# A hybrid DeltaNet and attention block: own buffers for the x rows, small rows on ACT's queue, early k-tiles four pieces sooner, block products of the two scan directions alternating

## What is computed

```python
shift, scale, gate = jnp.split((jax.nn.silu(c) @ w_mod + b_mod)[:, None, :], 3, axis=-1)
shift_c, scale_c, gate_c = jnp.split(jax.nn.silu(c_ctx) @ w_mod + b_mod, 3, axis=-1)
h = rms_norm(x, norm_w) * (1.0 + scale) + shift
hc = rms_norm(ctx, norm_w) * (1.0 + scale_c) + shift_c
aq, ak, av, az, ab, aa, bq, bk, bv, bz, br = split_in(h @ w_in)      # and the same for hc
# A: short conv, silu, l2 norm; gated delta rule in both directions, context first
#    each chunk solves (I + L) u = b v - ..., then o = q S + (q k^T decay) z, S <- g S + k^T z
# B: grouped-query attention with rotary positions over context and latent keys
x_new = x + gate * (sig(br_a) * (a_lat @ w_proj_a) + sig(br_b) * (b_lat @ w_proj_b)) @ w_out
```

## Time and profile before

| | us |
|---|---|
| median of 3 runs | 1854.47 |
| lowest and highest run | 1850.68, 1855.86 |
| the profiled execution | 1851.49 |
| its span, first to last instruction | 1849.2 |
| PE busy in the span | 1781.2 |
| DVE, ACT, POOL busy | 947.0, 661.9, 277.5 |

### The profile page before, as it was taken

The page is one execution under the profiler, slowest core; times in us unless marked ns, Lnnn a source line. Parts: engine busy times, 40 slices in busy tenths (PEclk is TensorE's granted clock), DMA queues, the critical chain, the costliest instruction groups (busy, mean ns, idle before and its releaser), DMA issues.

```text
span 1849.2 us, 25568 instructions
## 1 busy us (share of the span) xinstructions
PE 1781.2 (96%) x10286; PEld 1456.5 (79%) x10286; DVE 947.0 (51%) x1662; ACT 661.9 (36%) x1212; POOL 277.5 (15%) x421
## 2 busy tenths in 40 slices
PE   5799999999999999999999999999998999999999
PEld 2367888888787888878888888877877788788887
DVE  1244443456423566645555553764457876463334
ACT  4323331223233555535424345422246444222121
POOL 0000000000003356576100002111100110210000
PEclk9899999999999999999999999999999999999999
DMA  8794212223224566655444436767633332752332
GB/s 299 255 326 125 66 52 63 57 69 91 64 68 134 175 198 177 191 169 154 132 137 134 117 111 193 224 203 219 182 106 105 92 103 91 267 184 101 115 124 102
DMA packets 198685, 267.13 MB, mean 144 GB/s; under 512 B 37072, under 2 KB 135625, under 8 KB 197161
## 3 DMA queue, kind: packets, MB, share of 16 engines
q1 hardware_dynamic: 175241, 192.74, 34.7%
q0 software_dynamic: 15552, 58.62, 9.5%
q10 hardware_dynamic: 7776, 14.16, 2.1%
HBM read 221.96 MB, written 43.52 MB: 144 GB/s over the span
## 4 chain that ended last, share of the span: by engine, by line
PE 82%; DVE 7%; DMA 4%; ACT 4%; issue 2%; POOL 1%; SPq 0%; ACTq 0%; DVEq 0%; POOLq 0%
PE psum L1671 23%; PE psum L1673 22%; PE psum L1672 22%; PE psum L1819 2%; DMA w_raw_mod<-w_mod_dram 1%; PE psum L1768 1%; PE psum L1770 1%; DVE w_lo L1099 1%; PE psum L1664 1%; PE psum L1776 1%; ACT w_hi L765 1%; PE psum L1772 1%; PE psum L1774 1%; DMA w_raw<-w_proj_b_dram 1%; PE psum L1998 1%
## 5 line engine op out<-in xcount | busy, mean ns | idle before, releaser
L1099 DVE TENSOR_TENSOR w_lo<-w_raw,w_hi 128x1024 fp32r<-128x1024 f32 x232 | 291.0, 1254 | 593.0 <-ACT w_hi L765 592.7
L765 ACT ACTIVATE w_hi<-w_raw 128x1024 fp32r<-128x1024 f32 x232 | 245.7, 1059 | 861.6 <-PE psum L1673 772.3
L1671 PE MATMUL psum<-h_hi,w_hi 128*128 128x512 f32 x1152 | 469.6, 408 | 7.7 <-DVE w_lo L1099 5.4
L1672 PE MATMUL psum<-h_lo,w_hi 128*128 128x512 f32 x1152 | 451.6, 392 | 0.0
L1673 PE MATMUL psum<-h_hi,w_lo 128*128 128x512 f32 x1152 | 451.0, 392 | 0.0
L1671 PEld LDWEIGHTS psum<-h_hi,w_hi 128*128 128x128 f32 x1152 | 217.5, 189 | 67.0 <-issue 19.4
L1673 PEld LDWEIGHTS psum<-h_hi,w_lo 128*128 128x128 f32 x1152 | 216.9, 188 | 47.6
L1672 PEld LDWEIGHTS psum<-h_lo,w_hi 128*128 128x128 f32 x1152 | 217.8, 189 | 35.9
L1169 DVE SCALAR_TENSOR_TENSOR conv_acc<-conv_in,convw,conv_acc 128x772 f32<-128x772 f32 x96 | 98.2, 1023 | 3.4
L1671 PE MATMUL psum<-w_hi,m_hi 128*128 128x512 f32 x256 | 99.6, 389 | 0.0
L1672 PE MATMUL psum<-w_lo,m_hi 128*128 128x512 f32 x256 | 99.6, 389 | 0.0
(11 more groups left out here) (323 smaller groups left out, 2860.0 us busy)
## 6 DMA issues: line engine op xcount, KB each, us to landing
w_raw<-w_in_dram SPq DMA_DIRECT2D x168, 512.0 KB, 3.9
w_raw_mod<-w_mod_dram SPq DMA_DIRECT2D x64, 512.0 KB, 5.8
w_raw_modg<-w_mod_dram POOLq DMA_DIRECT2D x32, 512.0 KB, 4.7
w_raw<-w_out_dram SPq DMA_DIRECT2D x32, 512.0 KB, 3.7
gate_scratch<-gate_stage ACTq DMA_DIRECT2D x48, 256.0 KB, 4.3
w_raw<-w_proj_a_dram SPq DMA_DIRECT2D x16, 512.0 KB, 4.1
w_raw<-w_proj_b_dram SPq DMA_DIRECT2D x16, 512.0 KB, 3.5
gates<-gate_scratch POOLq DMA_DIRECT2D x32, 256.0 KB, 4.2
```

The source lines that it names most:

```text
L765: act.activation(part(whi[i % 2], p), part(place, p), ACT.Copy).then_inc(S("w_hi"), 1)
L1099: dve.tensor_tensor(part(wlo[i % 2], p), part(raw_of(n)[0], p), part(whi[i % 2], p).bitcast(f32), ALU.subtract).then_inc(S("w_lo"), 1)
L1671: pe.matmul(out_ap, lh, rh, start=first, stop=False, skip_group_check=shared)
L1672: pe.matmul(out_ap, lh, rl, start=False, stop=False, skip_group_check=shared)
```

## The change

1. Each of the six x tiles gets a buffer of its own, four of them in parts of `h_hi` and `h_lo` that aren't written yet. POOL loads tile t when tile t-2 has landed, and starts once the five transfers into `rows` have landed. A tile is taken up every two pieces instead of every three; its transposes come four pieces after its squares instead of three.
2. The ring of mod buffers has six places instead of four.
3. The six small transfers are issued by ACT instead of SP. PE waits for five of them; conv_rows is transposed after mod piece 3 and copied by DVE two pieces later.
4. Every early piece stands four mod pieces sooner (27, 35, 43, 51, 59 instead of 31, 39, 47, 55, 63), with its loads and splits. The conv piece after mod piece 63 (`BRIDGE`) gives its first k-tile before the last `mod_cols`.
5. `mod_cols` comes one piece later, at the second piece after a group's last one, `mod_columns` behind it; the first `h_columns` no longer waits until five pieces after the last x tile's squares.
6. In couple5, correct5, couple6 and correct6 PE first waits for both directions and then alternates between them head by head; `gp0` comes with the last but one product, `gp1` with the last.

```diff
-EARLY = {31: (0, 0), 39: (1, 0), 47: (0, 1), 55: (1, 1), 63: (0, 2)}
+EARLY = {27: (0, 0), 35: (1, 0), 43: (0, 1), 51: (1, 1), 59: (0, 2)}
...
+    BRIDGE = MOD_AT[63] + 1
+    BEFORE_LAST = {MOD_AT[63]: (BRIDGE, 0)} | {MOD_AT[m - 6 + 2 * kk]: (MOD_AT[m] + 1, kk) for m in EARLY for kk in range(3)}
     SPLIT_AT = [n - 1 for n in range(NP)]
     for m in EARLY:
-        SPLIT_AT[MOD_AT[m] + 1] = MOD_AT[m - 10]
-    SPLIT_AT[MOD_AT[63] + 2] = MOD_AT[59]
+        SPLIT_AT[MOD_AT[m] + 1] = MOD_AT[m - 8]
+    SPLIT_AT[BRIDGE] = MOD_AT[59]
...
-    X_AT = [1 + 3 * t for t in range(NT)]
-    H_AT = [max(g["last"] + 2, X_AT[-1] + 5) for g in MODS if g["scale"]]
-    H_AT[-1] -= 1
+    X_AT = [1 + 2 * t for t in range(NT)]
+    COLS_AT = [g["last"] + 2 for g in MODS[:-1]] + [MODS[-1]["last"]]
+    MODV_AT = [n + 1 for n in COLS_AT]
+    H_AT = [max(MODV_AT[gi], X_AT[-1] + 6) for gi, g in enumerate(MODS) if g["scale"]]
     H_PARTS_AT = [a + 1 for a in H_AT[:-1]] + [H_AT[-1]]
...
+    A_MODS = [A_H + 24576, A_H + 28672, A_H + 57344, A_H + 61440, A_C + 12288, A_C + 28672]
+    raw_mod = [at(f"w_raw_mod{i}", [P, 1024], a) for i, a in enumerate(A_MODS)]
+    RING_MOD = len(raw_mod)
...
+    A_X = [A_G + 49152, A_G + 57344, A_H + 8192, A_H + 16384, A_H + 40960, A_H + 49152]
+    xt = [at(f"x_rows{t}", [P, DM], a) for t, a in enumerate(A_X)]
...
         def _(pool):
+            pool.wait_ge(S("rows_in"), 80)
             for t in range(NT):
                 if t >= 2:
-                    pool.wait_ge(S("xt_ready"), 4 * (t - 1))
+                    pool.wait_ge(S(f"x_in{t % 2}"), 16 * (t // 2))
...
+                if k in ("couple5", "correct5", "couple6", "correct6"):
+
+                    for d in (0, 1):
+                        ready(d)
+                    for u in range(4):
+                        for d in (0, 1):
+                            ins = blocks(d, u)
+                            if u == 3:
+                                ins.then_inc(S(f"gp{d}"), 1)
+                    return
```

More of the change, by code:

```diff
@@ L1723, in scan, with ready @@
                     pe.wait_ge(S("k_rows"), N_UNITS)
-                for d in (0, 1):
-                    tile = pr["tiles"][d]
-                    b = 4 + 2 * d + i % 2
-                    ps = bank4(b)
+                def ready(d):
                     if i:
@@ L1742, in scan, with blocks @@
                         pe.wait_ge(S("k_rows_in"), 32 * (p + 1))
+                def blocks(d, u):
+                    b = 4 + 2 * d + i % 2
+                    if k == "couple6":
+                        r0, c0 = 64 * (1 - d), 64 * d
+                        return pe.matmul(bank4(b, 64)[c0:c0 + 64, u, :], LL[r0:r0 + 64, d, u, c0:c0 + 64],
+                                         YY[d][r0:r0 + 64, u, r0:r0 + 64], start=True, stop=True)
+                    if k == "correct6":
+                        c0 = 64 * d
+                        return pe.matmul(bank4(b, 64)[c0:c0 + 64, u, :], X64[c0:c0 + 64, u, :],
+                                         PM[c0:c0 + 64, u, :], start=True, stop=True)
+                    if k == "couple5":
+                        for c0, r0 in HALF_BLOCKS[d]:
+                            ins = pe.matmul(bank4(b, 32)[c0:c0 + 32, u, :], LL[r0:r0 + 32, d, u, c0:c0 + 32],
+                                            YC[d][r0:r0 + 32, u, :], start=True, stop=True)
+                        return ins
+                    for c0, r0 in HALF_BLOCKS[d]:
+                        pe.matmul(bank4(b, 32)[c0:c0 + 32, u, :], XC[d][c0:c0 + 32, u, :],
+                                  PM[c0:c0 + 32, u, 0:32], start=True, stop=True)
+                    c0, r0 = HALF_BLOCKS[d][d]
+                    return pe.matmul(other32(b)[r0:r0 + 32, u, :], PM[c0:c0 + 32, u, 0:32],
+                                     XC[d][c0:c0 + 32, u, :], start=True, stop=True)
@@ new lines, in scan @@
+                if k in ("couple5", "correct5", "couple6", "correct6"):
[7 more added lines that the diff above has]
+                    return
+                for d in (0, 1):
+                    tile = pr["tiles"][d]
+                    ps = bank4(4 + 2 * d + i % 2)
+                    ready(d)
@@ L1895, in _ @@
                 for t in range(NT):
-                    if n == X_AT[t] + 3:
+                    if n == X_AT[t] + 4:
                         x_transposes(t)
-                for gi, g in enumerate(MODS):
-                    if n == g["last"] + 1:
+                if n == X_AT[1]:
+                    pe.wait_ge(S("conv_rows_in"), 16)
+                    pe.transpose(bank(5, 120), crows[:], ident[0:120, 0:120]).then_inc(S("rowsT"), 1)
+                for gi in range(len(MODS)):
+                    if n == COLS_AT[gi]:
                         mod_cols(mrow, 6 + gi % 2, "mod", gi + 1)
```

70 lines of the change are left out of this document (24 added, 46 removed).

## The result

| | before | after |
|---|---|---|
| median of 4 runs each, us | 1855.2 (1850.7 to 1856.4) | 1828.7 (1825.4 to 1831.5) |
| ratio | | 0.9861, 95% interval 0.9837 to 0.9884 |
| profiled execution, us | 1851.5 | 1831.5 |
| its span, us | 1849.2 | 1828.9 |

The kernel became 26.5 us faster by the medians and 20.0 us by the two profiled executions, of which the one of after was the slowest of its four. The prediction was 1822.5 with a range of 1813 to 1836: the median lies in the range, 6 us above the number. Its two terms came out unlike each other: by its marks in the trace the opening brought more than was counted, the scan brought nearly nothing.

What follows compares the result with a forecast made beforehand. PE, busy 96% of the span, was taken to set the time after about 150 us, the opening being bound by late-starting transfers. Opening 20.9 plus scan 9.5 made 30.4 us less: 1822.5 us, between 1821.1 and 1824.1, range 1813 to 1836.

Steps and rivals of the forecast that it cites:

- the opening: Stretch up to the conv piece needing the last quarter of h: transfers start sooner, 20.9 us less (12 to 29).
- rival (a): Scan slots: the array gives nothing for alternating, or the gain turns into waits for both directions; 1832 us, chance 0.14.
- Where the time goes before: Whole kernel: PE's work sets the time after about 150 us; the opening is bound by transfers that start late.
- First k-tile: Opening: the first k-tile starts at 58 us instead of 80.3, with 18.9 MB loaded at 345 GB/s.
- First k-tile to the last mod piece: Opening: this stretch takes 74.8 us, 2.6 of it new stalls, so the last mod piece is used at 133 us.
- To the conv piece that needs the last quarter of h: End of the opening: 9.5 us after the last mod piece, starting at 142.5 instead of 163.4 us.
- Small rows on ACT's queue: Start of the kernel: mod pieces start 2.7 us sooner, PE at about 6.5 instead of 14.0 us; counted as nothing more.
- Scan: couple and correct slots: alternating directions overlaps products, 8.9 us in couple6 and correct6, 0.6 in couple5; 9.5 us in sum.
- (b): Opening: transfers don't come faster, rate near 309 GB/s or rows late; 12 instead of 20.9 us, 1831.5 us, chance 0.16.
- (d): Opening and scan: early k-tiles stall on h as long as they come sooner, slots stay; within 5 us of 1854, chance 0.03.
- (e): Scan slots: each change of direction drains the array, 63 us; 1896 us, slower from 0.073 us a change, chance 0.05.

Runs made afterwards that it cites:

- s2: The kernel after with the old scan function, so the new opening alone: 1831.8 us, ratio 0.9891 to before.
- o1: The kernel after with four instead of six mod buffers: 1842.5 us, ratio 0.9944 to before.
- o4: The kernel after with four mod buffers, the early pieces at their old places and the BRIDGE conv piece whole again: 1842.5 us, ratio 0.9948 to before.
- s1: The kernel before with the new scan function alone, opening unchanged: 1850.2 us beside 1850.8 for before, ratio 0.9995.
- s3: The kernel after, waiting for both directions first but running direction 0's products whole, then direction 1's, without alternation: 1837.9 us, ratio 0.9923 to before.
- s5: The kernel after with the wait for direction 1 moved behind two of direction 0's block products, correct6 alternating from the start: 1821.2 us, ratio 0.9823 to before.

## Why the prediction was right, and where its steps failed

**The time**: the median lies at the very edge of the forecast's own spread (1816 to 1829), and in part by luck. Of the two terms one is there and the other is almost wholly missing. The two halves as measured alone (0.0114 of 1853) would put the kernel at 1832 us, where rival (a) had it; the 4 to 5 us that the whole change shows above its halves have no known cause.

**Where the time goes before**: right. Only the opening had a high DMA rate and an unfilled PE; of the opening's gain of 22 to 23 us at the mark, s2 shows 19 in the time.

**First k-tile**, said for 58 us (54 to 63.5): 56.1 us, and 58.3 when it ran again. The bytes came faster than I took them, at 391 GB/s from 14 to 56 us against 345. The other chain, by the x tiles, was the later one, as the chain above shows from 41.9 us on. I had named it as equal, at 56.5 us. What I described in half a sentence ("six buffers keep requests queued") proved to be worth as much as the x buffers, ACT's queue and the new take-up together: 11.3 us from o1 to after, 8.6 us from before to o4. The last x tile landed at 37.8 us, said for 42.

**First k-tile to the last mod piece**: said 74.8 us, it took 130.0 - 56.1 = 73.9. The new waits for h_lo were said to be 1.3 us each and are 1.61.

**To the conv piece that needs the last quarter of h**: said for 142.5, it starts at 139.5 us instead of 163.4. Opening 23.8 us there, 20.9 predicted. In the time s2 shows 19.1 (17 to 23), so the term holds, and that it brought more than 20.9 is shown in the traces only.

**Small rows on ACT's queue**: PE starts its first mod piece at 9.1 us, not at 6.5, since five rows land at 8.1 us and not sooner. It was counted at nothing, and no kernel here moved it alone.

**Scan**, said to bring 9.5 us: this is the step that failed. s1 shows 0.6 us, the slots of the twelve pairs 1.6. The gain term was somewhat too large, 8.3 us measured against 10.7 (0.26 to 0.28 us in the 64-block slots instead of 0.4: they overlap, but not by half; 0.15 in couple5 instead of 0.1). The other term was mis-sized by more: I took 0.05 us for a wait that is met just when PE comes to it, since DVE's row ended at PE's start in the earlier trace rows, and the sum held 1.3 us for it (24 x 0.03 + 11 x 0.05). It costs 0.36, 0.12 and 0.22 us, 6.7 in sum. In the kernel before such a wait stood there too, but behind direction 0's 8 to 24 records, which hid it. The rows of before could not price it, and I took its cost from a coincidence of two time stamps. The order of the change on PE, which puts the wait for `gd1` ahead of the others ("waits gd1,diag,gd0"), stood in front of me; that each further wait instruction then costs 0.1 us, only the trace of after shows. Rival (a) said half of this, "their gain turns into waits for both directions", at 1832 us with the opening as predicted.

The prediction also drew on a rule. The Trainium skill (TensorE: Matmul & The Clock Gate, section "Wait — 56ns, not 53.3ns?") says that starts of matmuls never come closer than about 25 ns. This case's trace doesn't agree with it, and the measurement decides. The 32 records of couple5 (16 matmuls) take 0.45 us in after and 0.60 in s3, from the first start to the last end; a record lasts 0.19 us (the median), so from the first start to the last it is 0.26 and 0.41 us, 17 and 27 ns a matmul. By the rule couple5 should have gained nothing, and its products gained 0.15 us. correct5 gained 0.01, as the rule had it, but not because of a floor at 25 ns: its 24 matmuls start 18 ns apart in s3 and in after alike (0.55 and 0.54 us to the next k-tile, of which 0.12 us lie behind the last start). It used several places of the array within each direction already; that this is why it gained nothing wasn't tested.

**Rivals (b), (d), (e)**: the DMA rate rose (b falls), and the early k-tiles lost 1.6 us twice and not their lead (d falls). A change of direction costs less than nothing, not 0.073 us (e falls): alternating is cheaper in s3's comparison.

**The rest of the way.** At the scan's end after led by 24.3 us, at the end of the span by 20.3. The trace shows short stretches at half clock behind 180 us, up to the end of the span: 6.8 us in all in before, 17.1 in after, 13.7 in after's second execution, 8.7 in s5. In one place PE pauses in all four for 2.8 us, for a w_lo of DVE: the pause ends at 1219.6 us in before, 1195.6 in after, 1198.5 in after's second execution and 1188.6 in s5. Windows of 15 us around it (columns as in the earlier trace rows), in this order:

```profile
1214.00:1229.00 15.00, 11.30 (x49) 8.70 (x48) 14.18 (x32) 3.20 (x4) 1.43 (x2) 1.00 0.44 118
```

```profile
1190.00:1205.00 15.00, 12.21 (x42) 9.49 (x41) 12.74 (x30) 1.78 (x2) 1.42 (x2) 0.77 0.41 127
```

```profile
1193.00:1208.00 15.00, 11.30 (x49) 8.69 (x49) 14.18 (x32) 3.20 (x4) 1.43 (x2) 1.00 0.43 120
```

```profile
1183.00:1198.00 15.00, 12.20 (x47) 9.65 (x46) 13.66 (x31) 2.66 (x4) 1.43 (x2) 0.89 0.43 127
```

So the pause is no work of the change. The mean clock of the window is 0.77 in after and 0.89 in s5, while before and after's second execution keep the full clock (their windows hold a second pause of 0.9 us). At the pause's end after still leads by 24.1 us. At most half of a half-clock stretch is lost, so after lost up to 5 us more this way than before did, enough for the 4 us; no run shows that it was this. It differs between executions of one kernel. Whether the new opening makes such stretches likelier was not settled: o4 has as few of them as before, o1 more than after.

## What to carry to other kernels

Price a wait by what is queued in front of it on its own engine, and by how many more waits stand behind it: met with work in front it cost nothing here, met with an empty queue 0.12 to 0.36 us, even where the partner's row ends just then. So put short independent work ahead of the second wait instead of collecting all waits at the top (s5: 8.8 us faster than the version that collects them, 5.8 of them in its slots). Where the waits must be collected, let the one that is met last stand last. No kernel here tries this alone; an estimate from the 0.1 us for each wait instruction is 0.2 us in ten couple5 slots and 0.1 in eight latent couple6 slots, 3 us in all. When two streams share the DMA, size the ring of the one by the longest stretch in which its consumer is busy with the other, here two buffers of 512 KB for 9 to 11 us.

## What was unexpected about the hardware

- With an empty queue PE starts 0.15, 0.25 or 0.36 us behind the end of DVE's row, by whether none, one or two wait instructions stand behind the one for DVE; each took 0.10 to 0.11 us. The trace calls most of it issue, not a wait for DVE.
- 64x64 block products of two different quarters of the array take 0.61 us for eight when they alternate and 0.89 us when those of one quarter come in a row, start to the next k-tile.
- 32x32 block products that alternate between the directions start 17 ns apart in the mean (16 in 0.26 us), direction by direction 27 ns.
- The DMA held 391 GB/s for 42 us, more than the best 4 us of before, once six mod pieces and two x tiles stood in its queues; with four mod pieces it moved 324 GB/s in the same stretch.
- After one and the same pause of 2.8 us the granted clock fell to half in one execution and stayed full in another of the same kernel (windows above).
